# The projection to queries, keys and values: twelve plain tiles against six pairs by Strassen's products

## The reference, cut to what matters

```python
w_q, w_kv = w_qkv[j][:, :Q_WIDTH], w_qkv[j][:, Q_WIDTH:]          # 1024 x 1024 and 1024 x 512
q_l = apply_rope(attn_q(a_lat, w_q, g_q[j]), cos, sin)            # 8 heads of 128, 512 latent tokens
k_l, v_l = attn_kv(a_lat, w_kv, g_k[j]); k_l = apply_rope(k_l, cos, sin)   # 2 heads each
k_c, v_c = attn_kv(a_ctx, w_kv, g_k[j])                           # 256 context tokens, no rotation
k_all, v_all = concatenate([k_c, k_l]), concatenate([v_c, v_l])
s = q k_all^T / sqrt(128);  p = softmax(s);  o = p v_all          # 4 query heads share a key head
```

## Time and profile before

| | |
|---|---|
| median of three runs | 3538.63 us (3534.62 to 3538.77) |
| the profiled execution | 3537.2 us |
| its span | 3535.4 us |
| TensorE busy (PE) | 3248.2 us, 92% of the span |
| DVE, ACT, GpSimd busy | 1464.6, 976.3, 776.0 us |
| mean granted clock of TensorE | 0.966 of 2.4 GHz |

### The profile page before, as it was taken

How to read it: one execution, slowest core, us unless ns; L and a number is a source line. 1 busy time by engine, 2 the same in 40 slices (tenths; PEclk the granted TensorE clock), 3 DMA queues, 4 the chain that set the end, 5 groups by cost and what they waited for, 6 DMA issues and landing times. The chain is left out here.

```text
span 3535.4 us, 65390 instructions
## 1 busy us (share of the span) xinstructions
PE 3248.2 (92%) x26148; PEld 2151.9 (61%) x26148; DVE 1464.6 (41%) x3011; ACT 976.3 (28%) x1978; POOL 776.0 (22%) x726
## 2 busy tenths in 40 slices
PE   6998999999999999999999667879988899999987
PEld 3558555555555587788865357755775456666543
DVE  1124443345323455345358744434455233333324
ACT  2113222222002243222021445545322122222211
POOL 0000332233510014334520000004311233333320
PEclk9999999999999999999999689989999999999998
DMA  5320233312111003543211000001102799999996
GB/s 223 132 100 26 72 119 143 155 48 85 53 44 66 30 1 128 227 158 109 94 48 48 0 3 4 4 28 53 60 28 81 266 360 351 361 363 351 353 399 254
DMA packets 88110, 479.97 MB, mean 136 GB/s; under 512 B 16738, under 2 KB 20610, under 8 KB 42704
## 3 DMA queue, kind: packets, MB, share of 16 engines
q1 hardware_dynamic: 71504, 439.07, 33.5%
q0 software_dynamic: 16384, 37.72, 3.2%
HBM read 463.88 MB, written 29.36 MB: 140 GB/s over the span
## 5 line engine op out<-in xcount | busy, mean ns | idle before, releaser
L1010 PE MATMUL psum<-arena 128*128 128x384 f32 (+1 forms) x2464 | 674.7, 434 | 5.8 <-ACT arena L599 4.8
L1010 PEld LDWEIGHTS psum<-arena 128*128 128x128 f32 x2464 | 464.1, 189 | 220.8 <-issue 22.9
L841 PE MATMUL psum<-arena 128*128 128x256 f32 (+1 forms) x1904 | 511.9, 431 | 23.4 <-PEq L3153 10.1
L841 PEld LDWEIGHTS psum<-arena 128*128 128x128 f32 x1904 | 364.3, 192 | 171.4 <-issue 27.0
L3672 PE MATMUL psum<-arena 128*64 128x256 f32 x3072 | 352.4, 378 | 15.2 <-DMA arena<-exp_w_in 14.5
L3672 PEld LDWEIGHTS psum<-arena 128*64 128x64 f32 x3072 | 232.2, 134 | 160.2 <-issue 53.7
L452 POOL TENSOR_TENSOR arena<-arena 128x512 f32<-128x512 f32 x66 | 88.1, 1334 | 1037.4 <-POOLq L1653 348.5
L1138 DVE SCALAR_TENSOR_TENSOR arena<-arena 128x511 f32<-128x511 f32 (+1 forms) x264 | 176.9, 712 | 138.1 <-ACT arena L1116 135.0
L1088 ACT ACTIVATE arena<-psum 128x384 f32<-128x384 f32 (+1 forms) x176 | 76.3, 435 | 510.5 <-PE psum L1010 510.1
L461 POOL TENSOR_TENSOR arena<-arena 128x512 f32<-128x512 f32 (+1 forms) x74 | 114.7, 1550 | 395.4 <-PE psum L1010 245.6
L2524 ACT ACTIVATE arena<-psum 128x256 f32<-128x256 f32 (+2 forms) x456 | 158.1, 358 | 152.8 <-PE psum L2320 96.8
(11 more groups left out here) (485 smaller groups left out, 4942.3 us busy)
## 6 DMA issues: line engine op xcount, KB each, us to landing
arena<-exp_w_in SPq DMA_DIRECT2D x207, 1024.0 KB, 10.7
arena<-w_mod_r_in SPq DMA_DIRECT2D x72, 1024.0 KB, 7.0
arena<-w_ffn_up_in SPq DMA_DIRECT2D x44, 1024.0 KB, 4.8
arena<-w_ffn_down_in SPq DMA_DIRECT2D x32, 704.0 KB, 4.1
arena<-yrows SPq DMA_DIRECT2D x8, 2048.0 KB, 22.9
arena<-w_hgrn_in SPq DMA_DIRECT2D x10, 1024.0 KB, 4.7
arena<-w_even_in_in SPq DMA_DIRECT2D x17, 512.0 KB, 3.4
arena<-w_in_in SPq DMA_DIRECT2D x15, 512.0 KB, 3.3
```

The costliest lines, as they stand in the source:

```text
L841: mm = pe.matmul(pair_bank(ps, q, x, h), lhsT[:, k, :], rhs[:, k, :], start=(k == 0 and x in (1, 2, 7)), stop=(k == KH - 1), skip_group_ch ...
L1010: return pe.matmul(pair_bank(ps, q, x, h), feed.weights(m, q, x)[:, k, :], b.moving(x)[:, k, :], start=(k == 0 and x in (1, 2, 7)), stop=( ...
```

## The change

The twelve weight tiles become six pairs: the two keys, four pairs of queries, the two values last. The `Feed` becomes a `Pairs`, with 1 MB loads; the norm writes its activations in halves (`split=True`). Results go to a ring of four buffers `raw` in SBUF; squares, gain and rotation read them there. The keys' squares are summed by a full matrix of ones, which leaves the sum on all partitions, so that a logarithm and an exponential on ACT give the factor and no spreading is needed. The queries' root is taken in the same way, without the square root's table. The values are transposed by TensorE at the start of `attention`, behind the first two scores, and copied by ACT behind the first two exponentials.

```diff
-        qkv = Feed(nc, "qkv", io["w_qkv"], KD)
+        qkv = Pairs(nc, "qkv", io["w_qkv"])
...
+    b = Halves(m, m["A"], 4, T, NRM_RT, NRM_XN, QK_T4)
+    def width(i):
+        return LAT // 2 if 1 <= i < N - 1 else T // 2
+    def into(i, tile, half):
+        x = dst[:, 10 + tile, :] if i == N - 1 else raw[:, 2 * (i % 2) + tile, :]
...
         @block.tensor
+            def key_sums(n):
                 pe.wait_ge(s["sq"], n + 1)
+                if n:
+                    pe.wait_ge(s["klg"], n)
+                pe.matmul(ps[:, 6, :], m["ones"], sq[:, n, 0:LAT], start=True, stop=True)
+                pe.matmul(ps[:, 7, 0:CTX], m["ones"], sq[:, n, LAT:T], start=True, stop=True).then_inc(s["sm"], 1)
+            def query_sums(n):
+                pe.wait_ge(s["sq"], n + 1)
...
             norm.pe(pe, s)
+            for j, x in enumerate((1, 2)):
+                for k in range(4):
+                    pe.wait_ge(s["na"], 4 * j + k + 1)
+                    for i in range(2):
+                        mm = one(i, x, k)
...
+            for i in range(N):
+                if i >= 2:
+                    feed.arrived(pe, i, 0)
+                    pe.wait_ge(s["c12"], i - 1)
+                    product(i, 1)
+                    pe.wait_ge(s["c11"], i - 1)
+                    product(i, 2)
+                pe.wait_ge(s["ws"], 4 * i + 2)
+                pe.wait_ge(s["c1"], i + 1)
+                if i == 0:
+                    pe.wait_ge(s["tb"], 5)
+                product(i, 6)
+                if i >= 2:
+                    query_sums(2 * i - 2)
...
+                product(i, 7)
+                if i == 1:
+                    key_sums(0)
+                pe.wait_ge(s["c2"], i + 1)
+                product(i, 5)
+                if i >= 2:
+                    query_sums(2 * i - 1)
...
+                product(i, 4)
+                if i == 1:
+                    key_sums(1)
...
+                product(i, 3)
+        @block.gpsimd
+        def _(pool):
+            feed.sums(pool, m, s, 0)
+            b.first_sum(pool, s)
+            b.last_sum(pool, s, 5)
+            feed.last_sum(pool, m, s, 0)
+            for i in range(1, N):
+                feed.sums(pool, m, s, i)
+                feed.last_sum(pool, m, s, i)
         @block.scalar
+            for i in range(N):
+                if i >= 2:
+                    act.wait_ge(s["rope"], 2 * i - 2)
+                    copied(i, 1, 0, 0, "c1")
+                    if i == 2:
+                        key_roots()
+                copied(i, 6, 1, 0, "c2")
+                if i >= 1:
+                    squares(i - 1)
+                copied(i, 7, 1, 1, "c7")
+                if i == 1:
+                    key_logs(0)
+                copied(i, 3, 0, 1, "c12")
+                if i == 1:
+                    key_logs(1)
             act.wait_ge(s["sm"], 10)
-            act.activation(qroot, ps[:, 7, 0:32], ACT.Sqrt, scale=1.0 / P, bias=m["misc"][:, 0:1]).then_inc(s["qrt"], 1)
+            act.activation(qroot, ps[:, 6, 0:32], ACT.Ln, scale=1.0 / P, bias=m["misc"][:, 0:1]).then_inc(s["qrt"], 1)
+            act.wait_ge(s["qrt"], 1)
+            act.activation(qroot, qroot, ACT.Exp, scale=-0.5).then_inc(s["qrt"], 1)
         @block.vector
+            def rotated(n):
+                x, p, t = dst[:, head(n), 0:LAT], raw[:, n % 4, 0:LAT], t1[:, n % 2, :]
+                if n % 2 == 0:
+                    joined(dve, n // 2)
+                dve.wait_ge(s["sq"], n + 1)
+                dve.scalar_tensor_tensor(x, p, g, cos, MUL, MUL)
+                dve.scalar_tensor_tensor(t[lo, :], p[hi, :], g[hi, :], sin[hi, :], MUL, MUL)
+                last = dve.scalar_tensor_tensor(t[hi, :], p[lo, :], g[lo, :], sin[lo, :], MUL, MUL)
...
+                last.then_inc(s["rope"], 1)
...
             norm.dve(dve, s)
+            b.behind_norm(dve, s)
+            for i in range(N):
+                if i == 0:
+                    added(0, 2, 0, 0, "c1", "c11")
+                    added(1, 2, 0, 0, "c1", "c11")
+                if i >= 2:
+                    added(i, 2, 0, 0, "c1", "c11")
+                if i >= 1:
+                    rotated(2 * i - 2)
+                added(i, 5, 1, 1, "c7", "c22")
+                added(i, 4, 1, 0, "c2", "c21")
+                if i >= 1:
+                    rotated(2 * i - 1)
...
 def attention(nc, m, io, then):
             scores(0)
             scores(1)
+            for i in range(2):
+                for t in range(TT):
+                    mm = pe.transpose(ps[:, 4 + 2 * i + t // 4, t % 4 * P:(t % 4 + 1) * P], qkv[:, 10 + i, t * P:(t + 1) * P], m["ident"])
+                mm.then_inc(s["vt"], 1)
...
+                if g < 2:
+                    act.wait_ge(s["vt"], g + 1)
+                    act.activation(at(AT_V, 2, T)[:, g, :], pair_banks(ps, 2 + g, T), ACT.Copy).then_inc(s["vo"], 1)
```

More of the change, by code:

```diff
@@ L1715, in qkv_in, with head, joined @@
     sq, t1 = at(QK_SQ, 2, T), at(QK_T1, 2, LAT)
-    kroot, qroot = at(QK_ROOT, 12), at(QK_ROOT + 12, 32)
+    qroot, wide, raw = at(QK_ROOT, 32), at(QK_WIDE, 2, T), at(QK_RAW, 4, T)
     rq = at(AT_RQ, 2, 32)
+    b = Halves(m, m["A"], 4, T, NRM_RT, NRM_XN, QK_T4)
+    N = feed.n
     lo, hi = slice(0, 64), slice(64, 128)
     scale = float(P) ** -0.5
[L1720 to L1728, removed]
+    def head(n):
+        return 8 + n if n < 2 else n - 2
+    def width(i):
+        return LAT // 2 if 1 <= i < N - 1 else T // 2
+    def into(i, tile, half):
+        x = dst[:, 10 + tile, :] if i == N - 1 else raw[:, 2 * (i % 2) + tile, :]
+        parts = [(0, LAT // 2, 0)] + ([(LAT // 2, T // 2, LAT)] if width(i) == T // 2 else [])
+        return [(a, e, x[:, o + half * (e - a):o + (half + 1) * (e - a)]) for a, e, o in parts]
+    def joined(e, i):
+        for name in ("c11", "c12", "c21", "c22"):
+            e.wait_ge(s[name], i + 1)
     with st, nc.Block() as block:
@@ L1739, in _, with one @@
         def _(pe):
[L1740 to L1743, removed]
-                pe.wait_ge(s["sq"], n + 1)
-                for t in range(width(kind) // P):
-                    o = ps[:, 6, i * TT + t:i * TT + t + 1] if kind == "k" else ps[:, 7, 4 * i + t:4 * i + t + 1]
-                    mm = pe.matmul(o, sq[:, n % 2, t * P:(t + 1) * P], m["ones"][:, 0:1], start=True, stop=True)
+            def one(i, x, k):
+                h = width(i)
+                return pe.matmul(pair_bank(ps, i, x, h), feed.weights(m, i, x)[:, k, :], b.moving(x)[:, k, 0:h],
+                                 start=(k == 0 and x in (1, 2, 7)), stop=(k == 3), skip_group_check=x in (6, 5, 4, 3))
@@ new lines, in product @@
+            def product(i, x):
+                for k in range(4):
+                    mm = one(i, x, k)
+                mm.then_inc(s["mm"], 1)
+            def key_sums(n):
+                pe.wait_ge(s["sq"], n + 1)
+                if n:
[4 more added lines that the diff above has]
+                pe.wait_ge(s["sq"], n + 1)
+                if n == 2:
+                    pe.wait_ge(s["klg"], 2)
+                for t in range(LAT // P):
+                    mm = pe.matmul(ps[:, 6, 4 * (n - 2) + t:4 * (n - 2) + t + 1], sq[:, n % 2, t * P:(t + 1) * P],
+                                   m["ones"][:, 0:1], start=True, stop=True)
@@ L1748, in sums @@
                 mm.then_inc(s["sm"], 1)
             norm.pe(pe, s)
[L1751 to L1784, removed]
@@ L1787, in _, with copied, squares @@
+        @block.gpsimd
[7 more added lines that the diff above has]
+                feed.last_sum(pool, m, s, i)
         @block.scalar
         def _(act):
[L1789 to L1797, removed]
+            def copied(i, x, tile, half, name):
+                act.wait_ge(s["mm"], feed.made[i, x])
+                bank = pair_bank(ps, i, x, T // 2)
+                for a, e, to in into(i, tile, half):
+                    out = act.activation(to, bank[:, a:e], ACT.Copy)
+                out.then_inc(s[name], 1)
+            def squares(i):
+                joined(act, i)
+                for tile in range(2):
+                    n, w = 2 * i + tile, 2 * width(i)
@@ new lines, in key_roots @@
+            def key_roots():
+                for n in range(2):
+                    act.wait_ge(s["klg"], n + 1)
+                    act.activation(wide[:, n, :], wide[:, n, :], ACT.Exp, scale=-0.5).then_inc(s["krt"], 1)
+            norm.act(act, s)
+            copied(0, 1, 0, 0, "c1")
+            copied(1, 1, 0, 0, "c1")
+            for i in range(N):
[13 more added lines that the diff above has]
+                    key_logs(1)
```

102 lines of the change are left out of this document (56 added, 46 removed).

## The result

The changed kernel takes 3548.34 us (median of 9 runs, 3544.81 to 3549.46), the kernel before 3540.35 beside it: a ratio of 1.0022 with a 95% interval of 1.0013 to 1.0031. In a second comparison it was 1.0023 [1.0014, 1.0032]. So the change makes the kernel 0.2% slower, 8.0 us in the first comparison and 6.1 in the second, and the forecast of 3535.0 with its range to 3541 missed it on the wrong side; "slower" had been given 0.07. The two profiled executions differ by as much: span 3544.0 against 3535.4 us.

The account below looks back on a forecast made before the run. The prediction took the stage as TensorE's work laid end to end. A gain of 8.3 us, less 1.6 and 3.2 for clock falls, left 3.5 off the kernel before: 3535.0 us forecast, range 3528.5 to 3541.

Parts of the forecast that it names:

- something I don't list: Leftover case for any outcome outside the listed forecast and rivals, chance 0.04.
- Products, keys and values: In qkv_in: products in pairs save 13.0 us; keys and values shed one-column passes 2.4, spreading 3.1, transposes 1.7, adding 2.6.
- Head: Start of qkv_in: product 6 waits for the norm until 1098.4, 8.6 us of products done instead of 12; clock fall 1.6.
- Four waits: In query pairs 2 to 5, TensorE waits for ACT's copy and square behind product 6: 1.25 us each, 5.0 together.
- Clock: In qkv_in, two of four new waits halve TensorE's clock, costing 3.2 us; a fall in the head costs 1.6.
- Tail: End of qkv_in: 1.8 us behind the last product, then the barrier's 1.75; first scores at 1192.1 instead of 1200.73.
- Third rival: In qkv_in, DVE's rotation holds up product 6, 2.4 us late four times, 9.6 in all: 3544.7 us, chance 0.06.

Follow-up runs that it names:

- late sums: Changed kernel with the four sums of queries' squares moved behind the seventh product of a pair instead of the sixth: 3540.19 us, ratio 0.9999 to the kernel before.
- the kernel with 64 small matmuls: Changed kernel plus 64 unused matmuls of 32 x 32 weights and 8 columns in the first stage: 3548.39 us, ratio 1.0023 to the kernel before.
- late-sums kernel with 17 matmuls: Late sums plus 17 unused matmuls (68 instructions) in the first stage, scan starting 214 instructions into a load: 3547.39 us, ratio 1.0013 to the kernel before.
- experiment 4: The run of late sums: changed kernel with queries' sums behind the seventh product instead of the sixth; 3540.19 us, ratio 0.9999 to the kernel before.
- late-sums kernel at place 54: Late sums plus 41 unused first-stage matmuls, so the scan starts 54 instructions into a 256-instruction load: 3533.38 us, ratio 0.9979 to the kernel before.
- moved-back kernels: Changed kernel and late sums, each plus 41 unused first-stage matmuls (164 instructions): 3539.03 us (ratio 0.9997) and 3533.38 us (0.9979 to the kernel before).
- kernel before with 23 matmuls: Kernel before plus 23 unused matmuls (92 instructions) in the first stage's wait for weights: 3548.31 us, ratio 1.0023 to the kernel before.

## Why the prediction was wrong

**The step that failed** is in its first part: "A barrier stands at both ends, so whatever the stage gains reaches the end of the run." The barrier keeps buffers and semaphores apart, but not the places of TensorE's instructions: 91 more of them in two stages moved every load boundary behind. That cost the scan 6.9 and 8.7 us in stops in the two profiles of the changed kernel, of the 10.3 and 11.0 by which it grew. By the medians, the same shift costs the kernel before 8.0 us, and taking it back gives 7.4 (changed kernel) and 6.8 (late sums, across two comparisons: 3540.19 to 3533.38). The sum had no term for any later stage; it was under "something I don't list", 0.04.

The local steps, by their own numbers:
- **Products, keys and values**: right. At full clock 48 passes of 256 columns take 10.45 us (1134.98 to 1145.43 in the late-sums kernel), 0.218 each against 0.216. The sums of weights on GpSimd stayed hidden.
- **Head**: right in length. The seventh slice's passes began at 1098.00, 16.2 us behind the stage's first pass (1081.83), forecast 15.8, and product 6 eight passes later, at 1100.38, 18.6 behind, forecast 18.1. The gap of 2.71, forecast 2.9, left the clock at 1.00, so the 1.6 for a fall was not paid. In three of the six profiles that hold this stage unaltered the clock did fall in the head, behind the first gap of 2.11 (in the kernel with 64 small matmuls at 1090.0 us); product 6 still began 18.6 behind the first pass, since the slower passes only shortened the gap ahead of the seventh slice to 1.5. Only a fall behind the second gap was paid: in the late-sums kernel with 17 matmuls product 6 began 20.0 behind, and the stage took 1.4 us longer than the unpadded one's.
- **Four waits**: right in place and cause, 0.99, 0.99, 0.99 and 1.16 where 1.25 each was forecast: 4.13 for 5.0. At the first, ACT's copy began 0.04 us behind the end of the last pass (1129.89) where 0.2 was counted, its square 0.10 before the copy's end, and the way back took 0.05. The 0.2 was a misreading: it starts from the passes behind (1194.58), but the last product pass ended at 1187.62 + 7.12 = 1194.74, 0.04 ahead of ACT.
- **Clock**: two of four fell, as taken, in five of those six profiles, three in the sixth (that two is right is luck: two was a choice between none and four); experiment 4 removed the falls with the waits. The Trainium skill (TensorE: Matmul & The Clock Gate, "A second HAM failure mode: psum-queue depth-cycling") says that frequent short pauses between groups of matmuls can make the clock swing; here two or three of four did it, and one or two held in every profile.
- **Tail**: 2.36 us from the last product to the first scores, forecast 3.6. First scores 115.35 us behind the begin, forecast 116.6. They now start at full clock, where before the lower one lasted to 1203.6; half of the 2.9 us from 1200.73 on is 1.4 of the 2.1 that attention gained. I had counted none.
- **Third rival** (DVE late): didn't occur; nothing stands ahead of a later product.

Local gain 6.5, place of the code about 8 lost: that leaves 1.5 of the measured 6 to 8 us slower. About 5 us more (4.5 to 6.5) are lost, which moving the code back doesn't return (1.3 and 1.0 us gained then, not 6.5). The late-sums kernel at place 54 shows the like: its two stages gain 15.0 us, its total 8.8 and 8.4. In part it is the lower clock in the scan (above), and in the moved-back kernels the padding itself (the first stage ends at 43.0 and 44.0 us with 41 matmuls in the changed kernel, at 42.3 to 42.6 in the kernel before). `rwkv_gates` takes 78.1 to 78.6 us in every profile of a changed kernel against 77.1 to 77.5 before, and 77.9 in the kernel before with 23 matmuls, so some of that may be place too. All are seen, none is explained: the other engines' lists of instructions also became longer, and that wasn't tried. The cause of this part stays open.

## What to carry to other kernels

A gain in one stage doesn't add up to the end by itself: before believing a change of 0.2%, compare every stage's length, also of those whose code is the same. Where TensorE runs thousands of small matmuls, as in this scan, a few harmless matmuls in an earlier wait tell whether a loss is the change or the place of the code behind it. Put a reduction that waits for another engine's copy behind one more piece of TensorE's own work: here that gave 8.6 us of 115.5 in the stage.

## What was not expected of the hardware

- TensorE stops for up to 1.9 us at one fixed place in each 256 instructions, seen where small matmuls run through 256 in about 4.5 us (306.8 us by 68 loads). The next load's packet starts in the median 1.2 to 1.5 us behind that instruction and takes about 1.1 us, and a stop ends some 1.4 us behind the end of the packet before. Why the stop is at the 194th is not shown.
- What the stops cost depends on where in the scan they fall: 12.7 us between two of the five places tried in a scan of some 310 us (312.0 and 324.7), at the same work and with 49.2 and 46.0 us at the lower clock.
- 64 padding matmuls of 128 x 128 weights and 64 columns cost the first stage 10.7 us, the same number with 32 x 32 weights and 8 columns 1.5 (ends at 53.1 and 43.9 against 42.4).
